# Two gate blocks at every attention step, and GpSimd's waiting drain moved from the first joint block to the last

## The reference, cut to what matters

```python
def first_block(x, ...):
    p = _split_in(x @ w_in[l])
    ya = _mixer_a(p["a_q"], p["a_k"], p["a_v"], rpb_table[:, :A_HEADS])
    yb = _mixer_b(p["b_q"], p["b_ckv"], ...)
    ...
    gates = jax.nn.sigmoid(p["gate"].reshape(bsz, seq, N_BRANCHES, D_MODEL))
    merged = jnp.sum(gates * jnp.einsum('bsnc,ncd->bsnd', ys, w_branch[l]), axis=2)
    ...
    y = _moe(x, ...)
```

```python
def hybrid_layer(x, mem, ...):
    proj = rms_norm(x, norm_mix_g) @ w_in
    ...
    ret = bidirectional_retention(rq_h, rk_h, ...)
    na = neighbourhood_attention(...)
    mo = memory_attention(...)
    ...
    x = x + merged @ w_out
    a, g = jnp.split(rms_norm(x, norm_ffn_g) @ w_ffn_in, 2, axis=-1)
    return x + (jax.nn.silu(a) * g) @ w_ffn_out
```

## Time and profile before

| | us |
|---|---|
| median of 3 runs | 2688.27 |
| lowest, highest | 2683.43, 2690.13 |
| profiled execution, its own time | 2691.41 |
| its span in the profile | 2689.9 |
| TensorE busy in the span | 2585.6 (96%) |
| first attention, barrier to barrier (L341) | 165.0 to 257.4 |
| meeting between preparation and retention | PE idle 1191.5 to 1200.3 |
| last store has landed, last meeting begins | 2689.2 |

### The profile page before, as it was taken

The page is one execution under the profiler, slowest core; times in us unless marked ns, Lnnn a source line. Parts: engine busy times, 40 slices in busy tenths (PEclk is TensorE's granted clock), DMA queues, the critical chain, the costliest instruction groups (busy, mean ns, idle before and its releaser), DMA issues.

```text
span 2689.9 us, 30162 instructions
## 1 busy us (share of the span) xinstructions
PE 2585.6 (96%) x12456; PEld 1934.9 (72%) x12456; DVE 1075.9 (40%) x1764; ACT 787.0 (29%) x1125; POOL 948.5 (35%) x312
## 2 busy tenths in 40 slices
PE   8988889999889999989999999999999999999999
PEld 6765577788433336765888888888776888888887
DVE  4974553534421114367444411122376444311111
ACT  3034411422211113427222422322327222322221
POOL 4771100244023332320444444444321444444443
PEclk9988799999889999999999999999999999999999
DMA  4431000332769995320222222222420222222222
GB/s 170 161 136 61 20 32 1 118 110 79 294 227 390 387 385 226 136 81 8 103 94 94 95 99 105 94 94 94 136 89 26 101 94 94 94 94 96 103 100 78
DMA packets 82585, 336.28 MB, mean 125 GB/s; under 512 B 34214, under 2 KB 34598, under 8 KB 47248
## 3 DMA queue, kind: packets, MB, share of 16 engines
q1 hardware_dynamic: 47592, 308.16, 30.5%
q10 hardware_dynamic: 21032, 17.76, 2.2%
q0 software_dynamic: 13824, 8.44, 1.1%
HBM read 376.84 MB, written 28.74 MB: 151 GB/s over the span
## 4 chain that ended last, share of the span: by engine, by line
PE 52%; ACT 1%; DVE 1%; POOL 1%; issue 0%; ACTq 0%; POOLq 0%
PE bank L195 16%; PE bank L194 16%; PE bank L196 16%; PE bank L968 1%; PE bank L982 1%; PE bank L2926 1%; PE bank L2936 1%; POOL w_lo L168 1%; PE bank L953 0%; ACT att_p L1024 0%; PE bank L204 0%; PE bank L202 0%; PE bank L203 0%; ACT ha L3145 0%; DVE att_p L1092 0%
## 5 line engine op out<-in xcount | busy, mean ns | idle before, releaser
L168 POOL TENSOR_TENSOR w_lo<-w_raw,w_hi 128x2048 fp32r<-128x2048 f32 x149 | 693.8, 4656 | 1304.1 <-ACT w_hi L161 1285.2
L194 PE MATMUL bank<-xh,w_hi 128*128 128x512 f32 x1784 | 707.2, 396 | 14.8 <-DVE w_lo L432 11.1
L196 PE MATMUL bank<-xh,w_lo 128*128 128x512 f32 x1784 | 696.2, 390 | 0.0
L195 PE MATMUL bank<-xl,w_hi 128*128 128x512 f32 x1784 | 696.0, 390 | 0.0
L194 PEld LDWEIGHTS bank<-xh,w_hi 128*128 128x128 f32 x1784 | 336.1, 188 | 98.3 <-issue 25.1
L161 ACT ACTIVATE w_hi<-w_raw 128x2048 fp32r<-128x2048 f32 x151 | 288.3, 1910 | 370.9 <-PE bank L194 349.6
L195 PEld LDWEIGHTS bank<-xl,w_hi 128*128 128x128 f32 x1784 | 336.2, 188 | 74.1 <-issue 5.3
L196 PEld LDWEIGHTS bank<-xh,w_lo 128*128 128x128 f32 x1784 | 335.9, 188 | 69.9
L194 PE MATMUL bank<-ha,w_hi 128*128 128x512 f32 x480 | 186.7, 389 | 0.0
L195 PE MATMUL bank<-hb,w_hi 128*128 128x512 f32 x480 | 186.7, 389 | 0.0
L196 PE MATMUL bank<-ha,w_lo 128*128 128x512 f32 x480 | 186.7, 389 | 0.0
(11 more groups left out here) (588 smaller groups left out, 3749.1 us busy)
## 6 DMA issues: line engine op xcount, KB each, us to landing
w_raw<-weights SPq DMA_DIRECT2D x186, 1024.0 KB, 4.8
ring<-weights SPq DMA_DIRECT2D x49, 1024.0 KB, 14.1
before_halves<-weights SPq DMA_DIRECT2D x18, 1024.0 KB, 15.0
res<-weights SPq DMA_DIRECT2D x16, 1024.0 KB, 12.9
distance_bias<-distance_bias_once ACTq DMA_DIRECT2D x8, 512.0 KB
na_bias<-grid_bias ACTq DMA_DIRECT2D x16, 240.0 KB, 3.7
strips<-distance_bias SPq DMA_DIRECT2D x8, 448.0 KB, 3.9
ring<-picked_rows SPq DMA_DIRECT2D x6, 512.0 KB, 6.7
```

The source lines that it names most:

```text
L168: engine.tensor_tensor(self.lo[:, s, :], self.raw[:, s, :], self.hi[:, s, :].bitcast(F32), ALU.subtract).then_inc(self.split, 1)
L194: self.released(pe.matmul(out, hi, moving[0], start=start, stop=False))
L195: pe.matmul(out, hi, moving[1], start=False, stop=False)
L196: return pe.matmul(out, lo, moving[0], start=False, stop=stop)
```

## The change

Three things change. The table of blocks per step in the first attention was 3, 3, 2, 0 for s mod 4 = 0, 1, 2, 3, and is now 2 at each of the steps 0 to 15; the last three steps (16, 17, 18) have 3, 3, 2 as before. ScalarE's `gates.copy` was at the end of the steps 3, 7, 11, 15 and 19, and is now at the beginning of the steps 4, 8, 12, 16, and at the end of step 19. The first joint block is no longer drained, and the second one is.

```diff
                 if gates:
-                    gates.fill(pe, (3, 3, 2, 0)[s % 4])
+                    gates.fill(pe, 2 if s < 16 else (3, 3, 2)[s - 16])
...
             for s in range(steps + 4):
+                if gates and s and s % 4 == 0:
+                    gates.copy(act, 1, then_prepare=True)
                 if decays and s == 2:
...
-                if gates and s % 4 == 3:
-                    gates.copy(act, 1, then_prepare=s < 19)
+                if gates and s == steps + 3:
+                    gates.copy(act, 1)
...
     with ExitStack() as joint:
-        joint.enter_context(together(k, drained=True, met=True))
+        joint.enter_context(together(k, met=True))
         before = first_mixer_end()
 
         def meet():
             joint.pop_all().close()
-            joint.enter_context(together(k))
+            joint.enter_context(together(k, drained=True))
```

## The result

The changed kernel takes 2672.4 us (median of 7 runs, 2666.5 to 2678.7), the kernel before 2688.2 us (7 runs, 2683.2 to 2691.5). The ratio is 0.9947, with a 95% interval of 0.9929 to 0.9966; measured once more, beside other kernels, it is 0.9943 (0.9929 to 0.9957). The forecast was 2672.

A forecast was written before the change was run, and what follows sets the result against it. TensorE is busy for 96% of the span, so only its idle or lower-clock time pays. Attention 9.2, meeting 6.3 and clock behind it 0.7 sum to 16.2 us, off 2688.3: 2672 us, range 2664 to 2683.

The forecast's parts named there:

- The attention: First attention: placing blocks evenly shortens the stage by 9.2 us, bounds 4.8 (no clock gained) and 11 (all gained).
- Steps 12 to 15: First attention: full clock kept at step 12 gives 3.2 us, one block less in step 13 gives 0.67.
- Step 16: First attention: its blocks stay, but the clock stays up, so it falls from 6.50 to 4.03 us, 2.5 gained.
- Steps 8 to 11: First attention: one block less in each of steps 8 and 9, taken as worth 0.67 us each.
- Steps 4 to 7: First attention: step 4 gives 0.9 us with the clock lost, step 5 gives 0.6; blocks overrun by 0.2 before step 8.
- The meeting: Meeting before retention: without GpSimd's drain VectorE is last and TensorE begins 6.27 us earlier, bounds 5.5 and 6.5.
- The clock behind the meeting: First matmuls of retention: shorter TensorE idling partly spares the clock, worth 0.7 us, bounds 0 to 1.7.
- (a): First attention: clock falls as before, so it gives 4.8 us, with the meeting 11.1 in sum: 2677 us; chance 0.24.
- (b): First attention: added blocks delay the turns, so it gives 0 to 2 us, with the meeting 7 to 8: 2681; chance 0.09.
- (c): Program's end: GpSimd's drain ends only after the stores, giving back 7.9 us: 2680 us; chance 0.08.
- (d): First attention: thinly spread blocks leave it at half clock from step 1 on, 13 us slower, 2701; chance 0.04.
- (e): Attention and meeting: VectorE alone sets the waits and the meeting has another late comer, no change, 2688 us; chance 0.05.

## Why the prediction was right

**The attention: 9.2 us forecast; 7.9 in the profiled execution, 8.8 in the second profile of the same kernel, 9.1 by the times of the run with the blocks alone.** Over the eight profiles with this table the stage takes 81.5 to 84.4 us, 83.3 in the mean, where the forecast had 83. The mechanism is the forecast's: the blocks at the turns are free but for step 8, TensorE's steps 12 and 13 get shorter, and the clock holds at the steps 12 and 16. That the steps 8 and 9 get shorter too shows in a part of the profiles only. All profiles with two blocks at the steps 8 to 15 and the shift in place show steps 12 and 16 alike, to 0.02 us, with no half clock. The terms, by the profiled execution:

- The steps before 4 were put at 0.2 and gave 0.2; in three of the profiles they gave 1.5.
- Steps 12 to 15 were put at 3.2 + 0.67 = 3.9 us and gave 4.2, since step 12 fell to 2.96 us and not to 3.27.
- Step 16 was put at 2.5 and gave 2.95. Both terms were mis-sized because their full-clock price of 4.03 us was read at step 8 of the kernel before. There the six transposes came in two lots, the second behind a wait for VectorE's division, and took 1.17 us up to the outputs; at step 16 they come in one lot and take 0.77. That is 0.40 of the 0.48 us missed. So 4.03 is no price of the clock alone, and a stretch at half clock costs 2.9 us and not 2.46. The second lot, before:

```profile
204.95 0.55 PE L968 MATMUL bank<-consts,att_p 128*128 128x128 f32 x3 [0.18 <-DVE att_p L1099]
```

- Steps 8 to 11 were put at 1.3 and gave 0.8; in six of the other eight profiles with two blocks there and the shift in place they gave nothing (17.8 us). The "slack of half a microsecond" was not there: in those profiles TensorE waits some 1.2 us for ScalarE's copies in step 10. What made the wait is GpSimd: VectorE's masked additions of step 9 are stretched beside its work, and in the run without the shift the steps take 16.04 us with no wait.
- Steps 4 to 7 were put at 1.3 with the clock lost, and took 0.2 us longer. Step 4 itself gave 0.4, since the half clock covered all of it, and the rest was lost at the turn to step 8: VectorE was late in step 7 (the wait of 0.46 us at 200.50), and TensorE still had two blocks to do when it could have gone on. In the other nine profiles with two blocks there and the shift in place the half clock lasts 3.4 us, and these steps take 16.9 us in eight of them, 1.4 less than before, as forecast, and 17.8 in one. The forecast had costed a shift of the decays' addition against GpSimd's work at nothing, half a microsecond either way. That was too small: the addition and the operation ahead of it took 4.4 us together in the kernel before and in the profiled execution, and 1.7 to 2.3 in the others. How much of the 1.7 us between 18.6 and 16.9 this makes, and how much the longer half clock, is not shown.

**The meeting: 6.3 us forecast, 6.2 measured** (509.4 and 509.5 us with the drain, 503.3 in the changed kernel and with the drain alone moved), and VectorE is the last one there, as said.

**The clock behind the meeting: 0.7 us forecast, 0.5 measured** (1489.87 to 1489.41). It fell after 2.6 us of idle time too, but for a third as long.

**The end: nothing forecast, nothing measured**, by the run without a drain (1489.5 against 1489.4) and by the run that puts the drain late (5.9 us). The slack was forecast at 10.6 us and is 10.6.

**The base.** The forecast took all of it off the median of three runs, 2688.3; in the later comparisons the kernel before took 2690.8 and 2690.9. That the median came out within half a microsecond is in part luck, of the size of that difference; for the profiled execution the same sum was 3.5 us off (2675.2 against 2678.7), of which 2.8 lie in mixers C and D, where nothing was forecast.

**The rivals.** (a) the clock falls as before: false at steps 12 and 16, true at step 4, as the forecast had it, for 6.8 us in the profiled execution and 3.4 in the others. (b) the blocks do not come free: true in part at step 8 alone, as the forecast had it. (c) the drain's wait comes back at the end: the 7.9 us do come back there, but nothing waits for them. (d) thin blocks lose the clock: no step of the attention lost it that had it. (e) nothing changes: false, the whole interval of the ratio lies below 1.

## What to carry to other kernels

A filler on the in-order engine belongs in the step whose chain runs on other engines, and its gain is larger than the waiting it fills when that waiting cost the clock: here 5.7 of 9 us. A drain that must be paid once can be put where its engine has finished long before the others, and here one had to look for 8 us of slack there, not for a smaller price. Read a wait of one stage from two or more executions: here the same instructions took 16.9 or 18.6 us.

## What the runs showed of the hardware that was not expected

- GpSimd's drain took 7.9 us behind its last instruction in every first drain after the mixture of experts (those that start at 1186.9 and 2653.5 among them), and 7.9 us with no instruction of GpSimd's running when it began (2667.9). It took 0.07 us ahead of the mixture, 0.15 us in all behind one landed DMA of GpSimd's own, and 0.07 us when an earlier drain had been made after the mixture. By what else GpSimd did, the indirect DMAs are the likely cause; whether they as such or their number make it was not tried.
- The runs of one kernel are spread over up to 17 us (23 runs of the kernel before, 2679.1 to 2695.8), and the profiles show where most of it lies: mixers C and D, where TensorE is idle for short whiles all the time, took from 78.8 to 87.6 us with the same instructions. The granted clock over this stage for the kernel before, the changed one and the changed one again:

```profile
257.40:342.20 84.80, 68.29 (x288) 49.61 (x288) 46.08 (x75) 30.93 (x45) 9.78 (x4) 0.78 0.08 30
```

```profile
248.60:336.20 87.60, 69.27 (x288) 50.98 (x289) 47.42 (x75) 30.84 (x45) 9.46 (x4) 0.75 0.08 29
```

```profile
247.90:330.30 82.40, 64.04 (x288) 47.75 (x289) 47.19 (x75) 30.85 (x45) 9.47 (x4) 0.83 0.09 31
```

  From 0.75 to 0.83 is 5.2 us. So the 2.8 us that the profiled execution of the changed kernel lost there are of this kind, and most likely no effect of the change: over the eleven profiles with new tables and the shift in place the mean of this stage is 83.8 us, and 84.7 in both with the old one.
- Two VectorE operations of 128 x 512 took 0.69 us each without GpSimd's token shift, 1.67 and 2.74 us beside it in the profiled execution, and 0.69 and 1.64 in the second profile of the same kernel, where they met other parts of GpSimd's work. A masked addition of 128 x 256 took 0.42 and 2.16 us.
- TensorE's clock held after single waits of 1.08 and 1.52 us (steps 12 and 16) and of 1.37 us (step 4 without the shift), and fell after two waits of 1.0 to 1.5 and 1.4 us with 0.5 us of matmuls between them (step 4), and behind one of 2.62 us (the meeting).
